# Streaming encoder layer on one core: w_out of blocks 1 and 2 ahead of block 0's last query pairs, few dots around the layer norm, the last choice alone, tokens at tiles 70 and 94

## The reference

```python
h = x @ w_in                                  # one projection, split into q, k, v of two kinds of heads
mixed = concat(diff_attention(...), stick_breaking_attention(...))
x = layer_norm(ALPHA * x + mixed @ w_out)     # "LN1"
q = x @ w_q                                   # 8 PEER heads, 2 halves of 128
s = q . subkeys                               # 128 keys in each half
s1, i1 = top_k(s[:, :, 0], 16); s2, i2 = top_k(s[:, :, 1], 16)
top, pos = top_k(s1[..., :, None] + s2[..., None, :], 16)      # of 256 sums
g = softmax(top); e = expert index of pos     # out of 128 * 128 experts
act = gelu(x . peer_u[e]) * g
x = layer_norm(ALPHA * x + act @ peer_v[e])   # "LN2"
```

## Time and profile before

| what | us |
|---|---|
| median of three executions | 2603.69 |
| the profiled execution | 2600.89 |
| its span, first to last instruction | 2599.2 |
| TensorE busy (89% of the span) | 2306.4 |
| VectorE busy (56%) | 1468.4 |
| GpSimd busy (26%) | 678.5 |
| ScalarE busy (15%) | 377.4 |

### The profile page before, as it was taken

One profiled execution on the slowest core, in us unless ns is written; L12 is line 12 of the kernel. 1 busy time (PEld: TensorE's weight loads), 2 busy tenths in 40 slices (PEclk: granted clock), 3 DMA queues, 4 the chain that ended last, 5 costly groups with the idle time before them and its releaser, 6 DMA issues.

```text
span 2599.2 us, 29221 instructions
## 1 busy us (share of the span) xinstructions
PE 2306.4 (89%) x11802; PEld 1677.5 (65%) x11802; DVE 1468.4 (56%) x2342; ACT 377.4 (15%) x657; POOL 678.5 (26%) x470
## 2 busy tenths in 40 slices
PE   8999999988965498887497999999999999999990
PEld 8999999947622388886487999644444444444440
DVE  3333333353578978776785760255555555555568
ACT  3333333321000211000032320000000000000001
POOL 2000000000254534221401010143334443443452
PEclk9999999999987699999799999999999999999995
DMA  6434444365999799999989988999999999999994
GB/s 251 142 141 145 141 141 144 144 262 219 405 391 397 295 421 376 417 421 421 396 290 365 361 320 318 343 415 413 418 418 418 408 421 414 417 416 420 417 394 200
DMA packets 129924, 861.41 MB, mean 331 GB/s; under 512 B 14752, under 2 KB 14880, under 8 KB 33824
## 3 DMA queue, kind: packets, MB, share of 16 engines
q1 hardware_dynamic: 63360, 425.88, 41.9%
q0 software_dynamic: 56960, 408.97, 38.7%
q10 hardware_dynamic: 9504, 25.17, 2.5%
HBM read 833.75 MB, written 26.21 MB: 331 GB/s over the span
## 4 chain that ended last, share of the span: by engine, by line
DMA 41%; PE 34%; DVE 14%; issue 5%; POOL 4%; ACT 1%; DVEq 0%; SPq 0%; ACTq 0%; POOLq 0%
DMA scratch<-peer_v,idx_v 26%; DMA arena<-peer_u,idx_u 13%; PE bank L1250 9%; DVE scratch L1642 5%; PE bank L970 4%; PE bank L971 3%; PE bank L974 3%; PE bank L1233 3%; POOL arena L576 2%; PE bank L1092 2%; DVE arena L1581 2%; PE bank L992 2%; PE bank L988 2%; PE bank L989 2%; DMA cache<-u_tiles 2%
## 5 line engine op out<-in xcount | busy, mean ns | idle before, releaser
L1581 DVE CUSTOM_DVE_ANT_0 arena<-arena,x 128x2048 f32<-128x2048 f32 x256 | 583.1, 2287 | 171.5 <-DMA arena<-peer_u,idx_u 171.2
L576 POOL DMA_INDIRECT arena<-peer_u,idx_u x256 | 358.0, 1398 | 650.2 <-DVE dots L1581 601.6
L1642 DVE SCALAR_TENSOR_TENSOR scratch<-scratch,gate 128x2048 f32<-128x2048 f32 x112 | 263.3, 2351 | 378.7 <-DMA scratch<-peer_v,idx_v 378.0
L591 POOL DMA_INDIRECT scratch<-peer_v,idx_v x112 | 251.8, 2249 | 462.9 <-DVE scratch L1642 444.7
L1250 PE MATMUL bank<-scratch,cache 128*128 128x128 f32 x2048 | 242.3, 278 | 40.1 <-DMA cache<-u_tiles 40.1
L1293 DVE TENSOR_TENSOR arena_rounded<-arena,w_high 128x1024 fp32r<-128x1024 f32 x96 | 113.9, 1224 | 266.5 <-ACT w_high L658 266.5
L1250 PEld LDWEIGHTS bank<-scratch,cache 128*128 128x128 f32 x2048 | 235.8, 194 | 44.4 <-DMA cache<-u_tiles 44.4
L1250 PE MATMUL bank<-scratch,ln_rows 128*128 128x128 f32 x2048 | 239.1, 276 | 26.2 <-DMA ln_rows<-u_tiles 22.6
L1250 PEld LDWEIGHTS bank<-scratch,ln_rows 128*128 128x128 f32 x2048 | 232.6, 192 | 30.5 <-DMA ln_rows<-u_tiles 28.4
L1270 PE MATMUL bank<-ln_rows,scratch 128*128 128x512 f32 x512 | 230.3, 592 | 0.7 <-ACT scratch L837 0.7
L1270 PE MATMUL bank<-cache,scratch 128*128 128x512 f32 x512 | 230.2, 592 | 0.0
(11 more groups left out here) (209 smaller groups left out, 2843.4 us busy)
## 6 DMA issues: line engine op xcount, KB each, us to landing
ln_rows<-u_tiles SPq DMA_DIRECT2D x64, 1024.0 KB, 8.9
cache<-u_tiles SPq DMA_DIRECT2D x64, 1024.0 KB, 10.0
ln_rows<-peer_v SPq DMA_DIRECT2D x64, 1024.0 KB, 10.0
cache<-peer_v SPq DMA_DIRECT2D x64, 1024.0 KB, 9.1
arena<-w_heads SPq DMA_DIRECT2D x32, 1024.0 KB, 5.0
arena<-w_out SPq DMA_DIRECT2D x24, 1024.0 KB, 8.3
arena<-w_heads SPq DMA_DIRECT2D x8, 2048.0 KB, 8.6
arena<-w_q SPq DMA_DIRECT2D x16, 1024.0 KB, 9.0
```

The lines of the kernel that those rows point to most:

```text
L576: pool.indirect_dma_start(out=u_row[k % U_SLOTS], out_offset=None, in_=peer_u, in_offset=bass.IndirectOffsetOnAxis(ap=idx_u[:, p % 2, k:k ...
L591: pool.indirect_dma_start(out=v_row[slot], out_offset=None, in_=peer_v, in_offset=bass.IndirectOffsetOnAxis(ap=idx_v[:, q % 2, k:k + 1], a ...
L1581: dve.tensor_tensor_reduce(u_row[slot], u_row[slot], x1[:, 0 if p < H else 2, :], 1.0, 0.0, ALU.mult, ALU.add, dots[:, p % 2, k:k + 1]).th ...
L1642: dve.scalar_tensor_tensor(out=residual2, in0=v_row[slot], scalar=coef[:, GROUPS_DENSE + q, k:k + 1], in1=residual2, op0=ALU.mult, op1=ALU ...
```

## The change

The four parts of the title, and what goes with them:

- TensorE does block 0's query pairs 0 and 1, then the w_out pieces of blocks 1 and 2, then block 0's pairs 2 and 3. SyncE's queue follows that order, and pairs 2 and 3 use the ring of the other stages. Block 0's scores of pairs 1 and 2 get buffers of their own, so that their copies don't wait for a choice.
- ScalarE copies block 0's pairs 2 and 3 just ahead of ln1_deviation(1), and its gelus and exponentials are put elsewhere between the copies.
- VectorE does 2, 2, 3, 3, 2, 2 and 2 dots of place 1 between the steps of the additions and of LN1. Choice (0,2) with place 2, and place 3 alone, come behind it. Places 5 to 7 go with choices (1,0) to (1,2), choice (1,3) has no dots, and place 8 starts with the tokens.
- HOT_AT is (70, 94), and TOGETHER is 176.

```diff
-TOGETHER = H * K + 40
+TOGETHER = H * K + 48
-HOT_AT = (54, 78)
+HOT_AT = (70, 94)
...
+            for i in range(8):
+                if i < RING:
+                    sp.wait_ge(wo_used[1], 16 - RING + i + 1)
+                else:
+                    sp.wait_ge(query_done[0], 8 + i - RING + 1)
+                sp.dma_start(wq_slot[i % RING], w_q[8 + i]).then_inc(ring_loaded[i % RING], 16)
...
             activate(0)
-            activate(1)
-            for i in range(2):
-                copy_keys(0, 3, i)
-            gate_numerators(0, 2)
-            activate(2)
+            copies(2)
+            copies(3)
             ln1_deviation(1)
             ln1_scale(1)
             copy_x1T(1)
+            activate(1)
...
+            gate_numerators(0, 2)
             queries(0)
+            activate(2)
             queries(1)
+            activate(3)
+            queries(2)
+            queries(3)
             gate_numerators(0, 3)
             activate(4)
-            queries(2)
-            queries(3)
...
-            with pe.Fori(0, 4) as j:
+            with pe.Fori(0, 2) as j:
...
                 project_out(1, g, wq_slot[i % RING], out_banks(n))
+
+            for j in range(2, 4):
+                for i in range(2):
+                    for c in range(2):
...
+                        project_query(0, j, i, c, wq_slot[m % RING])
+                for i in range(2):
+                    score_keys(0, j, i)
...
             dots_and_choice(0, 0, 1)
-            dots_of(1, 0, 8)
+            dots_of(1, 0, 2)
             add_residual(1, 0, out_banks(0), 4)
-            dots_of(1, 8, 16)
+            dots_of(1, 2, 4)
             add_residual(1, 1, out_banks(1), 2 * 4)
-            dots_and_choice(2, 0, 2)
+            dots_of(1, 4, 7)
             add_residual(1, 2, out_banks(2), 3 * 4)
+            dots_of(1, 7, 10)
             add_residual(1, 3, out_banks(3), 4 * 4)
             ln1_moments(1)
-            dots_of(3, 0, 2)
+            dots_of(1, 10, 12)
             ln1_shift(1)
-            dots_of(3, 2, 6)
+            dots_of(1, 12, 14)
             ln1_affine(1, 0)
-            dots_of(3, 6, 10)
             ln1_affine(1, 1)
-            dots_of(3, 10, 16)
+            dots_of(1, 14, 16)
+            dots_and_choice(2, 0, 2)
+            dots_of(3)
             dots_and_choice(4, 0, 3)
-            for j in range(4):
+            for j in range(3):
                 dots_and_choice(5 + j, 1, j)
-            i = (H + 1) * K
+            choose(1, 3)
+            weigh(H - 1)
+            i = H * K
```

More of the change, by code:

```diff
@@ L425, in _ @@
                 sp.dma_start(wq_slot[i], w_q[i]).then_inc(wq_loaded[i], 16)
-            with sp.Fori(1, 4) as j:
-                for i in range(4):
-                    sp.wait_ge(query_done[0], (j - 1) * 4 + i + 1)
-                    sp.dma_start(wq_slot[i], w_q[j * 4 + i]).then_inc(wq_loaded[i], 16)
+            for i in range(4):
+                sp.wait_ge(query_done[0], i + 1)
+                sp.dma_start(wq_slot[i], w_q[4 + i]).then_inc(wq_loaded[i], 16)
             for i in range(16):
                 if i < RING:
-                    sp.wait_ge(query_done[0], 3 * 4 + i + 1)
+                    sp.wait_ge(query_done[0], 4 + i + 1)
                 else:
@@ L920, in _ @@
                             act.wait_ge(a_spilled, 32)
+                if t == HOT_AT[1] + P // HOT_PER_TILE + 4:
+                    activate(H + 1)
                 if t % A_CHUNK == A_CHUNK - 1:
@@ L927, in _ @@
                         if b and n == 2 * HOT_PER_DOT + 7:
-                            activate(TOGETHER // K - 1)
+                            activate(H)
                         if b == 0 and n == P - 1:
@@ L1582, in dot @@
                                          ALU.add, dots[:, p % 2, k:k + 1]).then_inc(u_dotted, 1)
-                if k == 3 and p > 0:
+                if k == 3 and p not in (0, H):
                     weigh(p - 1)
```

33 lines of the change are left out of this document (18 added, 15 removed).

## The result

The change makes the kernel faster by 4.5 us, where 11.5 were forecast. In one job, in turn on the same chip, the changed kernel took 2600.93 us (median of 20 executions, 2596.54 to 2607.98) and the kernel before 2605.43 us (median of 20, 2601.54 to 2609.23). The ratio is 0.9981, 95% interval 0.9973 to 0.9989, so the gain is small but clear of the spread. A second set gave 2600.76 us for the changed kernel and 0.998 (0.9969 to 0.999).

A forecast was written before the change was run, and what follows sets the result against it. DMA engines, full at 420 GB/s, were taken as the bound over most stretches. Terms -28, -22, +35, +36, +3, -19, then -2 and -9.5 made 11.5 us off the median: 2592 us, range 2571 to 2614.

The forecast's parts named there:

- slots: Units of 2.5 us, the DMA time of one dot's gather or one tile (1.049 MB) at 420 GB/s.
- Out-projection: w_out of blocks 1 and 2 starts at 646.81, chunk 2 at 730 instead of 758.17: 28 us earlier.
- Layer norm: LN1's root at 822, VectorE waiting from 795; queries of blocks 1 and 2 at 839.5 instead of 889.66, 50 us earlier.
- Queries: ScalarE holds up the query copies twice; TensorE waits 25 us, tiles start at 996 instead of 1011.3; 35 us given back.
- slower rival: Place 3's dots stay 4.97 us apart, its gelu comes at 983, tiles at 1018, total 2614 us; chance 0.18.
- Choices: The last choice ends at 1324 instead of 1303.0, 21 us later; tokens start at 1330 instead of 1305.83.
- The pause at tile 70: TensorE, at 4.63 us a tile, reaches tile 70 at 1314 and waits 10 us instead of 39.93.
- To the second pass: From tile 110 at 1557.5, 40 DMA slots take 100 us, plus 3.5; second pass starts at 1661 instead of 1655.6.
- the last stretch takes its gain back: Ahead of the second pass, tiles and gathers move at 374 GB/s, so 40 slots take 112 us: about 2603; chance 0.17.
- Second pass: Gathers of peer_v start at 1662; from there to the last add 889 us instead of 898.1, ending at 2551.
- Cross-check by empty slots: Unused DMA time summed over stretches: 59 us before against 46 after, 13 us, agreeing with the 11.5 forecast.
- The rate: Mixed tiles and gathers move at 420 GB/s up to the second pass, against the skill page's 358 for HBM loads.

The follow-up runs named there:

- ln_first: The changed kernel with LN1's root and scale of blocks 1 and 2 ahead of the copies of block 0's pairs 2 and 3 on ScalarE: 2578.97 us.
- gate_first: The changed kernel with the first two gatings ahead of the 26 dots that precede the second pass: 2600.62 us, 0.9977 of the kernel before.
- together40: The changed kernel with TOGETHER at H*K+40 instead of H*K+48, so 18 instead of 26 dots ahead of the second pass: 2598.08 us.
- choice_alone: The kernel before with only last choice without dots, tokens at 70 and 94, 48 dots before the second pass, four gelu chunks ahead of the first exponential: 2589.84 us.
- tokens54: The changed kernel with its tokens at tiles 54 and 78 instead of 70 and 94: 2639.49 us, 1.0127 of the kernel before.
- gelu3_late: The changed kernel with ScalarE's gelu of place 3 behind all query copies: 2617.60 us, 1.0046 of the kernel before.

## Why the prediction was wrong

The step that failed is a term of the chain, the last stretch ahead of the second pass: 40 slots and 100 us stood there, 103.5 us with the last dot and the gating, and it measured 44 slots and 114.3 us. With it the forecast had a span of 2588 us, and the trace has 2599.5. Step by step:

**Out-projection: right.** Chunk 2 starts at 727.73 (730 was forecast) behind a pause of 25.50 us, pairs 2 and 3 run from 784.34.

**Layer norm: right in time, and its weight was missed.** The root comes at 817.19 (822), the queries at 834.78 (839.5). The prediction saw that VectorE would wait at ln1_shift from 795 on. But it entered it as part of a gain (-22 against before) and didn't ask what the wait leaves empty, nor that two lines in another order would remove it. ln_first shows that it held 22 us, twice the whole forecast gain.

**Queries: right.** The exponential comes at 869.87 (873) and the gelu of place 3 at 958.47 (961), a pause of 27.69 us (25), tiles start at 994.38 (996). The slower rival, place 3 at 983, did not come about.

**Choices: right.** The last one ends at 1325.86 (1324), the tokens start at 1330.16 (1330). The pause at tile 70 was 0.85 instead of 10 us: from 994 to 1290 there are 1984 matmuls, 62 tiles, so one took 4.77 us and not 4.63, with the DMA full at 420 GB/s.

**To the second pass: the step that failed.** "14 tiles, 22 gathers, four tiles of the next pass, 40 slots, 100 us" was mis-sized. From 1557.25 to 1671.55 are 114.3 us where 103.5 stood. The DMA view above has 24.33 + 20.40 + 1.31 = 46.0 MB in that stretch, and 46.0 / 1.049 is 44 slots: 23.2 of gathers (24.33 MB), 19.5 of q1's (14 tiles of this pass and four of the next, one that was under way at 1557, and half a slot of the loads of a_kept), and 1.2 of spills. So by the bytes one gather, one tile, the loads and the spills had been left out. 44 slots at 420 GB/s take 110 us. The other 4.4 us are mostly dips of the rate: 333 and 52 GB/s in the two 3 us from 1557 on, 216 from 1668 to 1671, while the last dot and the gating run. The rival that the last stretch takes its gain back named the right place and size, 2603 us at 0.17, with the wrong cause: not a lower rate (374 against the 405 measured) but more slots.

**Second pass: right.** From the first gather of peer_v at 1674.55 to the last add at 2562.31 are 887.8 us (889).

So in the trace every step is in place but one, and that one takes the whole 11 us. The start of the second pass is not a cause in itself: gate_first moved it by 25 us and together40 by 21, and the end by 0.1 and 2.7. The forward chain was a way to count slots, and it had miscounted.

**Cross-check by empty slots: the right frame, left incomplete.** It set 59 us before against 46 after. The 46 held the layer norm, the last choice and the last stretch, and nothing for the queries, though the 59 had 11 for them. Measured in the rows above, 834 to 994 leaves 8.7, 2.8 and 10.0 us, 21.5 in all. The layer norm leaves 31 (728 to 834), the last choice 3.3, the last stretch 4.1, and 647 to 728 another 8.5. The whole ledger stands in the table: 135.1 before, 134.5 after. The changed kernel leaves 26 us more empty up to 1000, 10 less up to 1400 and 23 less up to 1680; the second pass has 6 more, of which the rounding of the rate allows 2. The 23 come from the second half of the change, since choice_alone has 25 less there by itself. The whole count gives a difference of 0.6 us, so that the incomplete one came to 13 us and agreed with the 11.5 of the chain was luck.

**The rate: right.** The stretch of choices and tiles ran at 420 GB/s, as the earlier trace rows said:

```profile
994.00:1290.00 296.00, 236.13 (x1984) 226.82 (x1984) 204.03 (x463) 19.58 (x30) 65.97 (x58) 0.99 1.01 420
```

The rule of the Trainium skill that was weighed ("DMA: Bandwidth & Descriptors", "Where 436 GB/s comes from", some 358 GB/s of loads per core) does not bind here, at 420 GB/s measured. The page "HBM Reference" of the Trainium skill, section "Specifications (TRN2)", has the case of this kernel, a core that streams alone, at about 425 GB/s, and with that this trace agrees.

**Still open:** the 4.5 us that the medians show and the two traces don't. The profiled execution of the kernel before was as much under its median, so its usual execution must be longer somewhere, and there is no trace of such an execution.

## What to carry to other kernels

Where the DMA engines are full for most of a kernel, write the ledger of DMA time left empty over *all* stretches, before and after, next to any chain. Here it accounts for the spans of 14 kernels to 6 us, while starting the second pass 25 us earlier, or taking away a pause of TensorE of 28 us, was worth 0 to 1 us. The ledger says what a gap costs, and the chain of waits says where an edit will make a new one: both are needed, as tokens54 and gelu3_late show. A pause costs if the transfers stop with it, since nothing uses up what they bring. So a wait of VectorE for a root that ScalarE has queued behind unrelated copies cost 22 us, and a wait of TensorE beside a busy DMA next to nothing. When a change has two halves, run each alone: here one half gave 18 us alone, and the other took some 12 of them back.
